# A retrieval layer's gate scatters: only the first head written plainly, seven heads added

## The chip, the cores and the metric

The kernel is one program on one NeuronCore of a Trainium2 chip. The metric is the device time of one execution in microseconds (us), lower is better. Its engines are TensorE (PE: matmuls, with PEld as its weight loads), VectorE (DVE), ScalarE (ACT), GpSimd (POOL) and SyncE (SP, which here only issues DMAs). The core's 16 DMA engines carry the transfers of all of them.

## The reference, cut to what matters

The program computes two transformer blocks over 512 tokens of width 1024. The change touches only the last layer of the second block, a retrieval layer with 16384 experts of one neuron each. Each of 8 heads picks 16 experts per token, with a softmax over its 16 scores as gates:

```python
s1, i1 = lax.top_k(s[:, :, 0], 16); s2, i2 = lax.top_k(s[:, :, 1], 16)
cand = s1[..., :, None] + s2[..., None, :]
cs, ci = lax.top_k(cand.reshape(..., 256), 16)
eidx = jnp.take_along_axis(cidx, ci, axis=-1)      # expert numbers, 0..16383
g = jax.nn.softmax(cs, axis=-1)
a = jax.nn.gelu(hid, approximate=False) * g
return jnp.einsum('chk,chkd->cd', a, vg)
```

Within a head the 16 experts of a token are different. Two heads may pick the same expert for a token, and then both gates count: their sum has to multiply that expert's hidden value.

## The kernel before, in words

**Dense with a gate matrix.** For the first three blocks of 128 tokens (`DENSE = 3`) the kernel doesn't gather rows of the expert tables. It computes the hidden values of all 16384 experts for all tokens, tile by tile (128 tiles of 128 experts), and multiplies them by a gate matrix `gates` in device memory, [expert, expert, token], that is zero wherever no head picked. The gate matrix is cleared early in the program. The fourth block of tokens takes its own way, by gathered rows, and isn't touched by the change.

**The gate scatter.** After each head's picks are known, GpSimd writes them into `gates`. One indirect DMA (`scatter(tb, k)`, lines 971 to 984) writes one element for each of 128 tokens: pick `k` of token block `tb`. A head is 3 x 16 = 48 such DMAs, the eight heads are 384. Line 980 is the plain form (it overwrites the element) for heads 0 to 3 (`PLAIN = 4`), line 983 the adding form (`compute_op=ALU.add`) for heads 4 to 7. The first DMA of a head waits for `s_tk`, which VectorE counts up when the head's gates are set; the first of each token block also waits until all scatters of the heads before it, for that block, have landed (`s_sc[tb]`). Ten scatters of head 0 are issued between GpSimd's last weight splits, the others follow in one sequence, head by head.

**Sums over equal picks.** A plain write overwrites what an earlier head left. So for heads 1 to 3 VectorE first looks up whether an earlier head picked the same expert for the same token, and adds that head's gate (`set_gates`, lines 2050 to 2061). For each of the three token blocks it compares the 16 picks with the 16, 32 or 48 picks of the heads before (line 2056), multiplies by their gates (line 2058), takes the maximum (line 2060) and adds it (line 2061). The copy `earlier` of the pick addresses is kept for this (line 2037).

**The phases around it.** The query projection (kind `wq`) and the key scores end the dense part of the program before this layer. Then comes the *hidden phase* (`hidden`, matmuls at line 1325): for each of 128 tiles, 24 matmuls over weights that SP loads (`load_u`), ScalarE rounds (`high_u`, line 1643) and VectorE completes with the low part (`low_u`, line 1954). ScalarE applies the gelu to the result (`kept_tile`, line 1378) and SP stores it (`keep`, lines 863 and 865). VectorE does the retrieval of heads 2 to 7 (`retrieve`) in the same time, in pieces between the `low_u` of the tiles; the order is written out by hand (`FIRST_LOWS_AT`, `LOWS_AT`): a head is 12 tiles long. ScalarE's exponentials for the softmax come at fixed tiles (`EXP_AT`). PE's code for the hidden phase is one unrolled round of four tiles and then a loop; the code of VectorE and ScalarE is unrolled until the retrieval is done. At the last hidden tile SP waits for all scatters (line 899) and loads the gates of the first four tiles (line 880). Then comes the *output phase* (`outputs`, line 1336), in which PE multiplies gated hidden values by the value table.

Of the kernel before, what the change touches and what calls it, by code (L numbers as in the profile page):

```python
# [24 lines left out]
U32 = mybir.dt.uint32  # L25
I32 = mybir.dt.int32
ALU = mybir.AluOpType
ACT = mybir.ActivationFunctionType
AX = mybir.AxisListType

P = 128
# [3 lines left out]
TB = T // P  # L35
# [11 lines left out]
TOPK = 16  # L47
NT = 128
DENSE = 3
TD = DENSE * P  # L50
PLAIN = 4
LOWS_AT = (1, 2, 1, 2, 1, 2, 1, 2)
FIRST_LOWS_AT = (0, 0, 0, 1, 2, 2, 1, 2)
EARLY = 2
# [348 lines left out]
def program(nc, t_in, out):  # L403
    build_schedule()
    ctx = ExitStack()
    with ctx:
        def sem(name):
            return ctx.enter_context(nc.semaphore(name))
# [40 lines left out]
        expert_gate = [region(o + 2 * P * tb + P, P) for tb in range(TB)]  # L449
        expert_lists = region(o, 2 * P * TB, TB)  # L450
# [57 lines left out]
        def rt(off, n, k=None):  # L508
            return region(TAIL + off, n, k, (tail, TAIL))
# [7 lines left out]
        eq = rt(15360, 1024)  # L517
# [10 lines left out]
        es = rt(19520, 16)  # L528
# [4 lines left out]
        picked = rt(19856, P)  # L533
        rated = rt(19984, P)
        token = rt(20112, 4)
        sum_before = rt(20116, TOPK)
        earlier = rt(20132, DENSE * TOPK * PLAIN, DENSE)
        gf = staged[:, 0:D]
        fss = staged[:, D:D + 16]
        fsq = staged[:, 2 * D:2 * D + 8 * T].rearrange("p (u n) -> p u n", u=8)  # L540
# [96 lines left out]
        s_tk = sem("topk_blocks_done")  # L637
# [41 lines left out]
        sq0, n = {}, 0  # L679
# [12 lines left out]
        auxi, n = {}, 0  # L692
# [45 lines left out]
        for n, (kind, _, loads) in enumerate(PROJ):  # L738
            if kind in SPLIT:
                same = users[kind == "br"]  # L740
# [193 lines left out]
        def _(pool):  # L934
# [36 lines left out]
            def scatter(tb, k):  # L971

                h = k // TOPK
                if tb == 0 and k % TOPK == 0:
                    pool.wait_ge(s_tk, h + 1)
                if h and k % TOPK == 0:
                    pool.wait_ge(s_sc[tb], 16 * k)
                where = bass.IndirectOffsetOnAxis(ap=expert_no[tb][:, k:k + 1], axis=0)
                if h < PLAIN:
                    nc.gpsimd.indirect_dma_start(gate_elements, where, expert_gate[tb][:, k:k + 1], None)\  # L980
                        .then_inc(s_sc[tb], 16)
                else:
                    nc.gpsimd.indirect_dma_start(gate_elements, where, expert_gate[tb][:, k:k + 1], None,  # L983
                                                 compute_op=ALU.add).then_inc(s_sc[tb], 16)
# [3 lines left out]
            for s in STEPS:  # L988
# [14 lines left out]
                elif s[0] == "mem_squares":  # L1003
                    k, mm_, total = s[1], dtmp[:, MEM:2 * MEM], dtmp[:, 0:MEM]
# [723 lines left out]
        def _(dve):  # L1728
            V = nc.vector
            chain = [0]  # L1730

            def link(ins):

                chain[0] += 1
                ins.then_inc(s_d, 1)
                dve.wait_ge(s_d, chain[0])
# [242 lines left out]
            def retrieve(h):  # L1979

                for w in range(2):
                    yield from sorted_half(2 * h + w)
                    yield
                c4 = cand.rearrange("p (t a b) -> p t a b", t=TB, a=16)
                ch = cand.rearrange("p (t n) -> p t n", t=TB)
                shape = [P, TB, 16, 16]
                link(V.tensor_tensor(c4, tva[:, :, 2 * h, :].unsqueeze(3).to_broadcast(shape),
                                     tva[:, :, 2 * h + 1, :].unsqueeze(2).to_broadcast(shape), ALU.add))
                numbers = tif.rearrange("p (t w m) -> p t w m", t=TB, w=2)
                link(V.tensor_copy(numbers, tia[:, :, 2 * h:2 * h + 2, :]))  # L1990
                for tb in range(TB):
                    ins = V.max(cs[:, tb, 0:8], ch[:, tb, :])
                link(ins)
                yield
                for tb in range(TB):
                    ins = V.max_index(ci[:, tb, 0:8], cs[:, tb, 0:8], ch[:, tb, :])
                link(ins)
                for tb in range(TB):
                    ins = V.match_replace(ch[:, tb, :], cs[:, tb, 0:8], ch[:, tb, :], -BIG)
                link(ins)  # L2000
                yield
                for tb in range(TB):
                    ins = V.max(cs[:, tb, 8:16], ch[:, tb, :])
                link(ins)
                V.tensor_tensor(ee[:, h, :].rearrange("p (t k) -> p t k", t=TB), cs,
                                cs[:, :, 0:1].to_broadcast([P, TB, 16]), ALU.subtract).then_inc(s_sm, 1)
                for tb in range(TB):
                    ins = V.max_index(ci[:, tb, 8:16], cs[:, tb, 8:16], ch[:, tb, :])
                link(ins)
                yield  # L2010
                cif = ci.rearrange("p t k -> p (t k)")
                for w in range(2):
                    if w == 0:
                        link(V.tensor_scalar(ca, cif, 4, None, ALU.logical_shift_right))
                    else:
                        link(V.tensor_scalar(ca, cif, 15, None, ALU.bitwise_and))
                    link(V.tensor_copy(cbf[:, w, :], ca))
                    q3 = eq.rearrange("p (r m) -> p r m", m=16)
                    q4 = eq.rearrange("p (t k m) -> p t k m", t=TB, k=16)
                    link(V.tensor_tensor(q3, cbf[:, w, :].unsqueeze(2).to_broadcast([P, 64, 16]),  # L2020
                                         iota16.unsqueeze(1).to_broadcast([P, 64, 16]), ALU.is_equal))
                    link(V.tensor_tensor(q4, q4, numbers[:, :, w, :].unsqueeze(2).to_broadcast(shape), ALU.mult))
                    link(V.tensor_reduce(sel[:, w, :], q3, AX.X, ALU.add))
                    if w == 0:
                        yield
                number, place = cbf[:, 0, :], cbf[:, 1, :]
                ks = slice(TOPK * h, TOPK * (h + 1))
                link(V.scalar_tensor_tensor(number, sel[:, 0, :], float(NKEYS), sel[:, 1, :], ALU.mult, ALU.add))
                for tb in range(TB):
                    part = slice(TOPK * tb, TOPK * (tb + 1))  # L2030
                    ins = V.tensor_scalar(place[:, part], number[:, part], float(TD if tb < DENSE else P),
                                          token[:, tb % DENSE:tb % DENSE + 1], ALU.mult, ALU.add)
                link(ins)
                places = place[:, 0:TOPK * DENSE].rearrange("p (t k) -> p t k", t=DENSE)
                link(V.tensor_copy(expert_lists[:, 0:DENSE, ks].bitcast(U32), places))
                if h < PLAIN:
                    link(V.tensor_copy(earlier[:, :, ks], places))
                link(V.tensor_copy(row_no[:, ks], number[:, TOPK * DENSE:]))
                link(V.tensor_copy(hidden_no[:, ks], place[:, TOPK * DENSE:]))

            def set_gates(h):

                dve.wait_ge(s_ex, h + 1)
                e3 = ee[:, h, :].rearrange("p (t k) -> p t k", t=TB)
                link(V.tensor_reduce(es[:, 0:4], e3, AX.X, ALU.add))
                link(V.reciprocal(es[:, 4:8], es[:, 0:4]))
                ks = slice(TOPK * h, TOPK * (h + 1))
                ins = V.tensor_tensor(expert_lists[:, :, P + TOPK * h:P + TOPK * (h + 1)], e3,
                                      es[:, 4:8].unsqueeze(2).to_broadcast([P, TB, 16]), ALU.mult)
                if 1 <= h < PLAIN:  # L2050
                    n = TOPK * h
                    shape = [P, TOPK, n]
                    same = eq[:, 0:TOPK * n].rearrange("p (k m) -> p k m", k=TOPK)
                    for tb in range(DENSE):
                        link(ins)
                        link(V.tensor_tensor(same, earlier[:, tb, ks].unsqueeze(2).to_broadcast(shape),  # L2056
                                             earlier[:, tb, 0:n].unsqueeze(1).to_broadcast(shape), ALU.is_equal))
                        link(V.tensor_tensor(same, same, expert_gate[tb][:, 0:n].unsqueeze(1).to_broadcast(shape),  # L2058
                                             ALU.mult))
                        link(V.tensor_reduce(sum_before, same, AX.X, ALU.max))  # L2060
                        ins = V.tensor_tensor(expert_gate[tb][:, ks], expert_gate[tb][:, ks], sum_before, ALU.add)  # L2061
                ins.then_inc(s_tk, 1)

            dve.wait_ge(s_kb[3], 16 * 4)
            link(V.tensor_tensor(eq[:, 0:P], ident, iota, ALU.mult))
# [1 line left out]
            for tb in range(1, DENSE):  # L2067
                ins = V.tensor_scalar(token[:, tb:tb + 1], token[:, 0:1], float(P * tb), None, ALU.add)
# [200 lines left out]
```

## Time and profile before

| | us |
|---|---|
| median of 3 runs | 2501.72 (2491.94 to 2502.61) |
| the profiled execution | 2497.29 |
| its span, first to last instruction | 2495.5 |
| PE busy | 2294.9 |
| POOL busy | 1163.1 |
| DVE busy | 1299.1 |
| mean granted TensorE clock | 0.961 of full speed |

Times in the rows below are from the start of the span. The hidden phase begins at 1156 us and ends at 1958 us. "PEclk" is the TensorE clock that was granted, as a share of full speed.

### The profile page before, as it was taken

How to read it: one execution, taken by the hardware profiler on the slowest of the kernel's cores; microseconds unless marked ns; L12 is line 12 of the kernel's file. 1: busy time of each engine (PE TensorE's matmuls, PEld its weight loads, DVE VectorE, ACT ScalarE, POOL GpSimd, SP SyncE). 2: the span in 40 equal slices, each digit the busy share in tenths (PEclk: the TensorE clock that was granted, in tenths of full speed). 3: DMA queues.
4: the chain of work that ended last, by engine and by line, in shares of the span. 5: the costliest groups of instructions: out<-in, count | busy, mean ns of one | idle time of the engine just before them, and what ended most of it. 6: DMA issues, size and time to landing. Idle time of an engine off the chain costs nothing.

```text
span 2495.5 us, 29790 instructions
## 1 busy us (share of the span) xinstructions
PE 2294.9 (92%) x9705; PEld 1779.3 (71%) x9712; DVE 1299.1 (52%) x2403; ACT 901.5 (36%) x1419; POOL 1163.1 (47%) x817
## 2 busy tenths in 40 slices
PE   7999999999999998975596599999999999999998
PEld 5666566787766766764385488888888788888887
DVE  4355433136323563874374366622222488888887
ACT  3554543336434443312121133322222333333333
POOL 3332121244432213375454658888820366555554
PEclk9999999999999999987697799999999999999999
DMA  6554233325321112211242167666643699999997
GB/s 211 190 191 135 70 90 103 95 87 186 114 76 60 43 35 84 70 58 39 64 139 88 55 147 147 144 145 145 135 108 108 228 330 341 355 349 358 355 357 249
DMA packets 208210, 392.32 MB, mean 157 GB/s; under 512 B 56160, under 2 KB 131936, under 8 KB 207872
## 3 DMA queue, kind: packets, MB, share of 16 engines
q1 hardware_dynamic: 151296, 323.89, 39.9%
q0 software_dynamic: 56832, 67.45, 10.8%
q8 instruction: 38, 0.62, 0.1%
q14 instruction: 44, 0.36, 0.0%
HBM read 330.21 MB, written 61.01 MB: 157 GB/s over the span
## 4 chain that ended last, share of the span: by engine, by line
PE 52%; issue 4%; another core or an unknown queue 3%; DVE 1%; ACT 1%; POOL 0%; DMA 0%; DVEq 0%; ACTq 0%; POOLq 0%
PE bank L1325 26%; PE bank L1336 20%; PE bank L1108 5%; PE bank L1304 1%; ACT u_tiles_split L1643 0%; POOL low L1027 0%; PE bank L1314 0%; DMA tail<-hidden_of_last_block,low 0%; DVE low L1784 0%; ACT staged L1378 0%; DVE h_low L1806 0%; DVE tail L2058 0%; DVE tail L2056 0%; DVE tail L2060 0%
## 5 line engine op out<-in xcount | busy, mean ns | idle before, releaser
L1325 PE MATMUL bank<-h_high,u_tiles_split 128*128 128x512 f32 x2048 | 643.8, 394 | 70.5 <-issue 43.9
L950 POOL TENSOR_TENSOR u_split<-blocks,u_split 128x1024 fp32r<-128x1024 f32 (+1 forms) x115 | 283.0, 2461 | 700.0 <-ACT u_split L1471 668.9
L1108 PE MATMUL bank<-h_high,u_split 128*128 128x512 f32 (+1 forms) x1712 | 567.3, 406 | 22.4 <-DVE h_low L1806 17.8
L1336 PE MATMUL bank<-v_split,a_split 128*128 128x512 f32 x2286 | 520.3, 390 | 4.6 <-DVE a_split L2096 4.6
L1325 PEld LDWEIGHTS bank<-h_high,u_tiles_split 128*128 128x128 f32 x2048 | 390.2, 191 | 162.1 <-issue 79.3
L1336 PEld LDWEIGHTS bank<-v_split,a_split 128*128 128x128 f32 x2286 | 430.1, 188 | 94.9 <-DVE v_split L2093 5.4
L1325 PE MATMUL bank<-h_low,u_tiles_split 128*128 128x512 f32 x1024 | 403.7, 394 | 14.6 <-issue 14.4
L1954 DVE TENSOR_TENSOR u_tiles_split<-tail,u_tiles_split 128x1024 fp32r<-128x1024 f32 x128 | 156.6, 1226 | 487.6 <-ACT u_tiles_split L1643 448.4
L1108 PEld LDWEIGHTS bank<-h_high,u_split 128*128 128x128 f32 (+1 forms) x1712 | 324.6, 190 | 110.9 <-issue 23.1
L983 POOL DMA_INDIRECT gates<-low x192 | 314.8, 1640 | 87.2 <-issue 58.2
L1108 PE MATMUL bank<-h_low,u_split 128*128 128x512 f32 (+1 forms) x728 | 287.9, 395 | 0.0
L1027 POOL DMA_INDIRECT low<-in_v,low x128 | 140.2, 1095 | 296.6 <-DVE low L2112 143.6
L980 POOL DMA_INDIRECT gates<-low x192 | 198.4, 1034 | 148.2 <-DVE low L2061 91.5
L1677 ACT CAST v_split<-tail 128x1024 fp32r<-128x1024 f32 x128 | 134.9, 1054 | 300.9 <-PE bank L1336 227.1
L1325 PEld LDWEIGHTS bank<-h_low,u_tiles_split 128*128 128x128 f32 x1024 | 195.4, 191 | 55.7 <-issue 15.7
L1378 ACT ACTIVATE tail<-bank 128x512 f32<-128x512 f32 x96 | 57.4, 598 | 451.3 <-PE bank L1325 223.4
L2093 DVE TENSOR_TENSOR v_split<-tail,v_split 128x1024 fp32r<-128x1024 f32 x128 | 157.0, 1227 | 69.2 <-ACT v_split L1677 56.4
L1035 POOL DMA_INDIRECT tail<-hidden_of_last_block,low x128 | 167.9, 1312 | 43.5 <-issue 38.7
L2112 DVE SCALAR_TENSOR_TENSOR low<-low,tail 128x1024 f32<-128x1024 f32 x128 | 163.8, 1279 | 1.6 <-DMA low<-in_v,low 1.3
L1108 PEld LDWEIGHTS bank<-h_low,u_split 128*128 128x128 f32 (+1 forms) x728 | 138.2, 190 | 33.0 <-issue 6.4
L1643 ACT CAST u_tiles_split<-tail 128x1024 fp32r<-128x1024 f32 x128 | 133.1, 1041 | 8.0 <-DMA tail<-in_uT 6.5
L1856 DVE TENSOR_REDUCE low<-bank 128x1 f32<-128x512 f32 (+3 forms) x112 | 59.7, 535 | 143.1 <-PE bank L1239 71.5
(201 smaller groups left out, 2474.9 us busy)
## 6 DMA issues: line engine op xcount, KB each, us to landing
tail<-in_uT SPq DMA_DIRECT2D x128, 512.0 KB
tail<-in_v SPq DMA_DIRECT2D x128, 512.0 KB
gates<-blocks SPq DMA_DIRECT2D x32, 768.0 KB, 5.8
tail<-gates SPq DMA_DIRECT2D x128, 192.0 KB
kept_hidden<-tail SPq DMA_DIRECT2D x96, 192.0 KB
tail<-kept_hidden SPq DMA_DIRECT2D x96, 192.0 KB
blocks<-in_r SPq DMA_DIRECT2D x24, 512.0 KB, 4.0
blocks<-in_conv SPq DMA_DIRECT2D x16, 512.0 KB, 4.2
```

The source lines that it names most:

```text
L950: nc.gpsimd.tensor_tensor(flat(u, 1)[:, 0:n], ring[:, loads[0] % NW, 0:n], flat(u, 0)[:, 0:n].bitcast(F32), ALU.subtract).then_inc(s_wlo, 1)
L980: nc.gpsimd.indirect_dma_start(gate_elements, where, expert_gate[tb][:, k:k + 1], None)\
L983: nc.gpsimd.indirect_dma_start(gate_elements, where, expert_gate[tb][:, k:k + 1], None, compute_op=ALU.add).then_inc(s_sc[tb], 16)
L1027: nc.gpsimd.indirect_dma_start(rows_in[:, k % 4, :], None, v_rows, bass.IndirectOffsetOnAxis(ap=row_no[:, k:k + 1], axis=0))\
L1035: nc.gpsimd.indirect_dma_start(picked[:, k:k + 1], None, hidden_elements, bass.IndirectOffsetOnAxis(ap=hidden_no[:, k:k + 1], axis=0))\
L1108: last = mm(ps[0:m, :], flat(u, part)[:, k * m:(k + 1) * m], x, start=(k == 0 and j == 0), stop=(k == nk - 1 and j == 2))
L1325: last = mm(bank[slot % 2][:, :], U4[:, slot, w, k, :], x[:, k, :], start=(k == 0 and x is hh and w == 0), stop=(k == KD - 1 and w == 1))
L1336: done = mm(bank[2 + 2 * tb + dh][:, :], A2[:, slot, wa, tb * P:(tb + 1) * P], V2[slot // 2][:, slot % 2, wv, dh * T:(dh + 1) * T], start= ...
L1677: nc.scalar.copy(V2[slot // 2][:, slot % 2, 0], VR[:, slot, :]).then_inc(s_vhi, 1)
L1954: V.tensor_tensor(U4[:, slot, 1].rearrange("p k e -> p (k e)"), UR[:, slot, :], U4[:, slot, 0].rearrange("p k e -> p (k e)").bitcast(F32), ...
L2093: V.tensor_tensor(V2[slot // 2][:, slot % 2, 1], VR[:, slot, :], V2[slot // 2][:, slot % 2, 0].bitcast(F32), ALU.subtract).then_inc(s_vlo, 1)
L2112: V.scalar_tensor_tensor(sparse, rows_in[:, slot, :], rated[:, bass.ds(k, 1)], sparse, ALU.mult, ALU.add).then_inc(s_axpy, 1)
```

## The change

`PLAIN` goes: only head 0 is written plainly, heads 1 to 7 are all scattered with the adding form. VectorE's comparison with earlier heads and its copy of the addresses are taken out.

```diff
@@ def scatter(tb, k)
-                if h < PLAIN:
+                if h == 0:
                     nc.gpsimd.indirect_dma_start(gate_elements, where, expert_gate[tb][:, k:k + 1], None)\
                         .then_inc(s_sc[tb], 16)
                 else:
@@ def retrieve(h)
-                places = place[:, 0:TOPK * DENSE].rearrange("p (t k) -> p t k", t=DENSE)
-                link(V.tensor_copy(expert_lists[:, 0:DENSE, ks].bitcast(U32), places))
-                if h < PLAIN:
-                    link(V.tensor_copy(earlier[:, :, ks], places))
+                link(V.tensor_copy(expert_lists[:, 0:DENSE, ks].bitcast(U32),
+                                   place[:, 0:TOPK * DENSE].rearrange("p (t k) -> p t k", t=DENSE)))
@@ def set_gates(h)
-                ks = slice(TOPK * h, TOPK * (h + 1))
-                ins = V.tensor_tensor(expert_lists[:, :, P + TOPK * h:P + TOPK * (h + 1)], e3,
-                                      es[:, 4:8].unsqueeze(2).to_broadcast([P, TB, 16]), ALU.mult)
-                if 1 <= h < PLAIN:
-                    n = TOPK * h
-                    shape = [P, TOPK, n]
-                    same = eq[:, 0:TOPK * n].rearrange("p (k m) -> p k m", k=TOPK)
-                    for tb in range(DENSE):
-                        link(ins)
-                        link(V.tensor_tensor(same, earlier[:, tb, ks].unsqueeze(2).to_broadcast(shape),
-                                             earlier[:, tb, 0:n].unsqueeze(1).to_broadcast(shape), ALU.is_equal))
-                        link(V.tensor_tensor(same, same, expert_gate[tb][:, 0:n].unsqueeze(1).to_broadcast(shape),
-                                             ALU.mult))
-                        link(V.tensor_reduce(sum_before, same, AX.X, ALU.max))
-                        ins = V.tensor_tensor(expert_gate[tb][:, ks], expert_gate[tb][:, ks], sum_before, ALU.add)
-                ins.then_inc(s_tk, 1)
+                V.tensor_tensor(expert_lists[:, :, P + TOPK * h:P + TOPK * (h + 1)], e3,
+                                es[:, 4:8].unsqueeze(2).to_broadcast([P, TB, 16]), ALU.mult).then_inc(s_tk, 1)
```

## Rows read from the trace of the kernel before

**Rows 1.** The page: PE over the span, and its granted clock in 40 slices.
```profile
PE 2294.9 (92%) x9705; PEld 1779.3 (71%) x9712; DVE 1299.1 (52%) x2403; ACT 901.5 (36%) x1419; POOL 1163.1 (47%) x817
...
PEclk9999999999999999987697799999999999999999
```

**Rows 2.** Busy time by stretch: start:end, length, engines, granted clock, DMA share, GB/s.
```profile
1098.00:1148.00 50.00, 8.31 (x40) 6.92 (x38) 7.46 (x45) 1.69 (x3) 33.91 (x36) 0.61 0.02 1
1156.00:1180.80 24.80, 24.75 (x108) 20.34 (x109) 19.84 (x48) 8.83 (x14) 18.67 (x18) 1.00 0.35 96
1180.80:1225.60 44.80, 12.33 (x26) 6.79 (x26) 1.23 (x1) 1.53 (x2) 30.24 (x31) 0.58 0.07 18
1225.60:1296.40 70.80, 70.80 (x307) 58.47 (x307) 55.81 (x151) 27.40 (x34) 22.92 (x20) 0.98 0.48 145
1296.40:1336.20 39.80, 18.21 (x66) 12.59 (x64) 9.41 (x44) 2.26 (x5) 28.43 (x29) 0.72 0.14 40
1336.20:1386.60 50.40, 49.49 (x207) 40.46 (x208) 40.26 (x99) 16.33 (x21) 18.77 (x17) 0.95 0.48 146
1386.60:1432.20 45.60, 16.68 (x53) 11.50 (x52) 11.42 (x45) 2.81 (x3) 30.82 (x32) 0.68 0.11 29
1455.80:1640.00 184.20, 184.20 (x814) 152.56 (x814) 118.63 (x328) 61.45 (x77) 155.90 (x93) 1.00 0.68 145
1640.00:1828.90 188.90, 188.90 (x835) 156.48 (x834) 42.23 (x38) 53.87 (x70) 158.92 (x99) 1.00 0.66 138
```

**Rows 3.** Who waited for whom, 1180 to 1226 us: us in total, times, longest.
```profile
PE bank L1325 <- issue: 32.4, 14, 17.5
DVE u_tiles_split L1954 <- issue: 31.3, 1, 31.3
```

**Rows 4.** DMA, all queues, 1180 to 1210 us.
```profile
DMA packets 768, 0.01 MB, mean 0 GB/s; under 512 B 768, under 2 KB 768, under 8 KB 768
```

**Rows 5.** DMA, 1450 to 1750 us: all queues, then GpSimd's queue alone.
```profile
DMA packets 45248, 43.50 MB, mean 145 GB/s; under 512 B 24096, under 2 KB 38176, under 8 KB 45243
...
q0 software_dynamic: 21456, 0.09, 19.6%
```

**Rows 6.** POOL in order of time: start, us; first and last scatter of head 1, of heads 4 to 7.
```profile
1156.95 1.69 POOL L980 DMA_INDIRECT gates<-low  x1 [14.37 <-DVE low L2061]
...
1219.23 0.95 POOL L980 DMA_INDIRECT gates<-low  x1 [0.31 <-issue]
...
1455.86 2.36 POOL L983 DMA_INDIRECT gates<-low  x1 [28.99 <-DVE low L2048]
...
1827.37 1.55 POOL L983 DMA_INDIRECT gates<-low  x1 [0.30 <-issue]
```

**Rows 7.** Matmuls of the hidden phase alone (line 1325), by stretch.
```profile
1156.06:1432.22 276.16, 192.25 (x763) 0.82 0.29 86
1640.00:1828.90 188.90, 188.90 (x835) 1.00 0.66 138
```

**Rows 8.** DVE, 1150 to 1460 us, by line and shape: busy us, mean ns.
```profile
L2056 DVE TENSOR_TENSOR tail<-tail 128x768 f32<-128x768 f32 x3 | 2.9, 958 | 0.1
...
L2056 DVE TENSOR_TENSOR tail<-tail 128x512 f32<-128x512 f32 x3 | 2.1, 692 | 0.1
...
L2061 DVE TENSOR_TENSOR low<-low,tail 128x16 f32<-128x16 f32 x9 | 1.6, 174 | 0.3
L2056 DVE TENSOR_TENSOR tail<-tail 128x256 f32<-128x256 f32 x3 | 1.3, 425 | 0.1
```

**Rows 9.** SP's queue in order of time: the loads of the first four gate tiles.
```profile
1954.24 1.78 SPq L880 DMA_DIRECT2D tail<-gates  x4
```

**Rows 10.** All scatters of the adding form: ns min/median/max, first and last start.
```profile
L983 POOL DMA_INDIRECT gates<-low x192: 1552/1559/2612, 1455.9 to 1827.4; - x192
```

**Rows 11.** DVE in order of time: retrieval work from one low part to the next.
```profile
1292.21 0.19 DVE L2016 TENSOR_SCALAR tail<-tail 128x64 uint32<-128x64 uint32 x1
...
1301.77 1.23 DVE L1954 TENSOR_TENSOR u_tiles_split<-tail,u_tiles_split 128x1024 fp32r<-128x1024 f32 x1
```

More of the change, by code:

```diff
@@ L50 @@
 TD = DENSE * P
-PLAIN = 4
 LOWS_AT = (1, 2, 1, 2, 1, 2, 1, 2)
@@ L535, in program @@
         token = rt(20112, 4)
-        sum_before = rt(20116, TOPK)
-        earlier = rt(20132, DENSE * TOPK * PLAIN, DENSE)
         gf = staged[:, 0:D]
```

## The prediction

> **What bounds the kernel now.** I read the page first. PE is busy for 92% of the span, and its clock row is at 9 everywhere except in five slices in the middle, where it falls as low as 6 [rows 1]. So PE sets the time, and the place to look is the one where it is not running. I then asked for busy time by stretch around those slices, moving the borders until each stretch held either a running or a halting PE. The hidden phase falls apart into stretches of two kinds [rows 2]. In three of them (44.8, 39.8 and 45.6 us long) PE does 26, 66 and 53 matmuls at a mean granted clock of 0.58 to 0.72. In the others it does 24 matmuls, one tile, in about 5.5 us. There is one more such halt ahead of the phase, from 1098 to 1148 us, with 40 PE instructions in 50 us.
>
> What does PE wait for there? The view of waits names no engine: the largest entries of PE and of DVE are "issue" (PE 32.4 us in 14 pieces, DVE 31.3 us in one piece) [rows 3]. Every compute engine but POOL stands still at once: DVE 1.23 us of work in 44.8, ACT 1.53, while POOL is busy 30.24 [rows 2]. The DMA view of 30 us inside it shows 768 packets that carry 0.01 MB, nothing else: the loads and stores of the phase have stopped too [rows 4]. POOL's timeline says what these packets are. It issues the plain scatters of head 1 from 1156.95 to 1219.23, 48 of them in 62 us [rows 6]. The halt begins some 24 us after the first and ends some 5 us after the last. The second and third halt lie in the same way in heads 2 and 3, and the 50 us ahead of the phase in head 0.
>
> The contrast is in the same trace. From 1455.86 to 1827.37 POOL issues the 192 scatters of heads 4 to 7, the adding form [rows 6]. The two stretches that hold them show PE at 184.20 of 184.20 and 188.90 of 188.90 us, at clock 1.00, beside 138 to 145 GB/s [rows 2]. GpSimd's queue takes 19.6% of the DMA engines there, for 0.09 MB [rows 5], so these writes are not free, but nothing waits for them. Nor is it the form of the code: PE has been in its loop since the fifth tile, and the code of VectorE and ScalarE is still unrolled at head 4 and 5, while DVE is busy for 118.63 of 184.20 us [rows 2]. I conclude that the plain element scatters, at this rate, halt the chip's other queues, and the adding ones don't. What exactly in the chip fills up, the trace doesn't show.
>
> **The change, step by step.** The sum is made against the profiled execution, 2497.3 us; the median of the runs is 4.4 us above it.
>
> *The halts of heads 1 to 3 go.* From the first hidden matmul to the end of the third halt, 276.16 us, PE does 763 matmuls [rows 7]. The undisturbed rate is 188.90/835 = 0.2262 us [rows 7], the same with busy DVE (184.20/814 = 0.2263) [rows 2]. 763 of them take 172.6 us. The halts and their slow clock cost 276.2 - 172.6 = 103.5 us. For the adding form at heads 1 to 3 there is no row; the bounds are no halt (the 373 us of adds at heads 4 to 7) and the same halt (plain at heads 1 to 3). I take no halt, because the nearest rows are the same instruction, the same 48 per head, beside the same loads and the same VectorE work.
>
> *The scatters get slower.* A plain scatter follows the last after (1219.23 - 1156.95)/47 = 1.33 us, an adding one after (1827.37 - 1455.86)/191 = 1.945 us [rows 6]. Beside a busy DVE it is 184.20/93 = 1.98 [rows 2]. POOL gets 144 x 0.65 = 94 us more. Nobody waits for a single scatter; what waits is SP, which at the last hidden tile needs all of them before it loads gates, now at 1954.24 [rows 9]. With the phase 103.5 us shorter that is 1850.7. Head 1's gates are set 4.4 us earlier (next step), so its first scatter is at 1152.5. 144 at 1.98 end at 1437.6, where head 4's gates are long ready: by the order in `LOWS_AT` they are set behind the low part of tile 25, at the latest near 1156 + 27 x 5.43 = 1303. Then 192 at 1.945 end at 1811. That leaves 40 us. This is cover, not gain: behind the scatters POOL has only work that waits for the last hidden tile anyway. Without the cover each 0.1 us per scatter would cost 34 us.
>
> The Trainium skill (SBUF — State Buffer, the section on its two separate sides) warns that GpSimd is kept from writing DMA descriptors while VectorE uses the port pair that they share. By that the scatters beside the retrieval would be spaced out more. The trace bears it out by little: 1.98 us beside the busy DVE against 188.90/99 = 1.91 beside the idle one [rows 2].
>
> *VectorE loses the sums.* Per token block there are three passes and a short add: three blocks at 16, 32 and 48 earlier picks are 3 x (3 x 0.425 + 0.174) = 4.4, 3 x (3 x 0.692 + 0.174) = 6.8 and 3 x (3 x 0.958 + 0.174) = 9.1 us [rows 8]; the passes of lines 2058 and 2060 are taken to be as long as that of 2056. With some 0.2 us for each of four copies this is 21 us. I count it as nothing. It hides behind matmuls: in the stretch that holds head 2's sums PE runs 70.80 of 70.80 us and DVE 55.81 [rows 2]. Only head 3's, the longest, may have cost PE the 0.9 us that it lacks in the next running stretch, which the 103.5 already contain.
>
> *What doesn't move.* Head 0 stays plain, so the 50 us before the phase stay. The output phase has the same work. The sum is 2497.3 - 103.5 = 2393.8; I say 2394.
>
> **The rivals.**
>
> *VectorE comes late once PE doesn't halt (0.10).* Its longest stretch of retrieval between two low parts is 1301.77 - 1292.21 = 9.6 us [rows 11], longer than a tile of 5.4. If nothing were made ahead, heads 2 and 3 would lose 4.2 us each and the start of the retrieval in the phase some more: about 2402 to 2410. Against it: heads 4 to 7 have the same order and lose nothing [rows 2].
>
> *The adds halt partly (0.05).* In heads 1 to 3 half of the gain is kept: 2394 + 52 = 2446. For it: they follow at once on head 0's plain writes, which no row shows. Against it: head 4's adds follow head 3's plain writes after 29 us [rows 6] and PE stays full.
>
> *POOL becomes the bound (0.04).* The scatters end after SP needs them when one takes more than (1850.7 - 1152.5)/336 = 2.08 us, against 1.945 to 1.98 now: at 2.2 us the time is 2394 + 41 = 2435. To cost more than before takes over 2.38 us each. The longest single add took 2.61 us [rows 10]; with 0.30 of issue between two, 336 of these would give 2394 + 279 = 2673, the far bound. The rows of heads 4 to 7 hold 192 of them, busy and idle neighbours included, and none of the stretches is near 2.08.
>
> *The adds halt everything as well (0.05, the other side).* If the small writes as such are the cause, a head's halt grows with its scatters. Halts now cost 34.5 us per head; adds take 30 us longer per head, all of it behind the first 24 us, so each halt becomes 64 us: 2497 + 90 = 2587. It decides as soon as the adds of a head halt for longer than the plain ones did. The Trainium skill (DMA: Bandwidth & Descriptors, Specifications) speaks for this: transfers under 512 B are done by reading, modifying and writing, which would make plain and adding elements alike. The rows of heads 4 to 7 contradict it as a cause of halts.
>
> **How the numbers follow.** The forecast has 0.76: 2394, its own range 2384 to 2404 (the runs before scatter by 11 us). The range of 8 in 10 adds the late VectorE and a part of the partial halt: 2380 to 2430; above it lie most of the partial halt, half of the POOL-bound case and the other side, some 0.12, below it 0.02. About 0.5%, 12 us, is what a measurement can tell from no change. Faster takes the first four cases without the POOL-bound tail: 0.94. The other side and that tail give slower 0.05, and 0.01 is left for no difference.
>
> **What would show it.** PE runs without a break from 1156 us on, and the hidden phase ends near 1854. Only 48 plain scatters are left, with one halt at 1098 to 1148. The adds follow each other every 1.9 to 2.0 us, from about 1152 to 1811, and SP's first gate load comes near 1851, not later than the last tile asks. PE's clock row loses its dip but for head 0's slices. It is wrong if PE's "issue" waits come back in heads 1 to 3, if SP's gate load waits for the last scatter, or if PE waits for line 1954 in the first 20 tiles.

## The result

| | kernel before | changed kernel |
|---|---|---|
| median, us | 2496.83 (2487.37 to 2502.61, 4 runs) | 2399.56 (2396.45 to 2403.02, 4 runs) |
| the profiled execution, us | 2497.29 | 2401.24 |
| its span, us | 2495.5 | 2399.4 |
| mean granted clock | 0.961 | 0.976 |

The ratio is 0.9614, 95% interval 0.9576 to 0.9653. On this occasion, whose chip isn't known, the change saves 97 us. The experiments ran on four chips that are named below by their numbers, and on three of them there was nothing to save: there the kernel before itself takes 2347 to 2349 us. So the profile after is read first as it is, and then the other chips.

**The page of the changed kernel:** PE over the span and the granted clock. Of the dip of five slices [rows 1] two slices are left.

```profile
PE 2277.0 (95%) x9705; PEld 1772.5 (74%) x9712; DVE 1273.5 (53%) x2363; ACT 901.0 (38%) x1419; POOL 1256.1 (52%) x817
...
PEclk9999999999999999997799999999999999999999
```

**Changed kernel, busy time by stretch** (start:end, length, PE, PEld, DVE, ACT, POOL, clock, DMA share, GB/s). These answer to [rows 2].

```profile
1098.00:1148.00 50.00, 15.61 (x79) 13.94 (x77) 13.31 (x49) 5.59 (x8) 38.53 (x38) 0.63 0.03 1
1148.00:1164.70 16.70, 0.00 (x0) 0.00 (x0) 0.00 (x0) 1.09 (x3) 13.96 (x10) 0.50 0.23 0
1164.70:1351.60 186.90, 186.86 (x815) 154.59 (x816) 121.79 (x368) 63.82 (x82) 157.95 (x96) 0.99 0.65 139
1351.60:1535.00 183.40, 183.40 (x811) 151.84 (x810) 119.42 (x330) 60.86 (x77) 155.36 (x93) 1.00 0.67 144
1535.00:1803.00 268.00, 268.00 (x1184) 221.93 (x1183) 60.66 (x52) 75.41 (x98) 223.88 (x139) 1.00 0.63 131
```

PE runs without a break through the stretches that hold the adds of heads 1 to 3, beside as busy a VectorE as before. The halt of head 0 has stayed, and it has grown: it now lasts until 1164.7, and in its last 17 us no compute engine but POOL does anything worth the name. DMA share is 0.23 there with 0 GB/s: from 1149 to 1163 us all 1152 packets are GpSimd's, so what the DMA engines do is adds.

**Changed kernel, the chain that ended last** (the work that set the time, each piece followed back to what released it). The whole hidden phase is one piece of 3072 matmuls.

```profile
1138.71 24.89 another core or an unknown queue
1163.61 1.08 ACT low L1660 x2
1164.74 698.64 PE bank L1322 x3072
```

**Changed kernel, POOL and SP in order of time:** the last plain scatter, the first and the last add, the first loads of gates. They answer to [rows 6, 9].

```profile
1143.98 0.96 POOL L977 DMA_INDIRECT gates<-low  x1 [0.30 <-issue]
1145.25 1.62 POOL L980 DMA_INDIRECT gates<-low  x1 [0.30 <-issue]
...
1799.40 1.57 POOL L980 DMA_INDIRECT gates<-low  x1 [0.32 <-issue]
...
1859.53 1.78 SPq L877 DMA_DIRECT2D tail<-gates  x4
```

The mean time between starts is (1799.40 - 1145.25)/335 = 1.953 us, and the scatters end 58 us before SP asks for them.

**The balance of the two profiled executions.** The hidden phase takes 698.6 instead of 1958.13 - 1156.06 = 802.1 us: -103.4. It begins at 1164.7 instead of 1156.1: +8.7. What lies behind it takes 536.0 instead of 537.4: -1.4. The sum is -96.1 us, and 2497.3 - 2401.2 = 96.1.

### The profile page after: what moved, and what is told of

Same layout as the page of the kernel before. It is cut to its first block, busy times and chain, and to the rows that moved or that the text cites. A ratio compares the mean times of both kernels' runs of the same rounds, so it can differ in the third digit from the quotient of the medians.

```text
span 2399.4 us, 29750 instructions
## 1 busy us (share of the span) xinstructions
PE 2277.0 (95%) x9705; PEld 1772.5 (74%) x9712; DVE 1273.5 (53%) x2363; ACT 901.0 (38%) x1419; POOL 1256.1 (52%) x817
## 4 chain that ended last, share of the span: by engine, by line
PE 55%; another core or an unknown queue 3%; DVE 1%; ACT 0%; POOL 0%; issue 0%; DMA 0%; DVEq 0%; POOLq 0%
PE bank L1322 29%; PE bank L1333 21%; PE bank L1105 5%; PE bank L1301 1%; POOL low L1024 0%; DMA tail<-hidden_of_last_block,low 0%; DVE low L1781 0%; ACT staged L1375 0%; DVE h_low L1803 0%; ACT u_tiles_split L1640 0%; POOL tail L1032 0%; DVE low L2126 0%; PE bank L1189 0%; ACT blocks L1375 0%
## 5 line engine op out<-in xcount | busy, mean ns | idle before, releaser
L1322 PE MATMUL bank<-h_high,u_tiles_split 128*128 128x512 f32 x2048 | 632.3, 390 | 22.3 <-ACT low L1660 22.3
L980 POOL DMA_INDIRECT gates<-low x336 | 553.6, 1648 | 102.4 <-issue 102.4
L1322 PEld LDWEIGHTS bank<-h_high,u_tiles_split 128*128 128x128 f32 x2048 | 385.4, 188 | 102.7 <-ACT low L1660 22.5
L1951 DVE TENSOR_TENSOR u_tiles_split<-tail,u_tiles_split 128x1024 fp32r<-128x1024 f32 x128 | 156.9, 1226 | 420.4 <-ACT u_tiles_split L1640 410.6
L1024 POOL DMA_INDIRECT low<-in_v,low x128 | 145.5, 1137 | 221.4 <-DVE low L2093 135.1
L2074 DVE TENSOR_TENSOR v_split<-tail,v_split 128x1024 fp32r<-128x1024 f32 x128 | 157.0, 1226 | 68.0 <-ACT v_split L1674 53.0
L1468 ACT CAST u_split<-blocks 128x1024 fp32r<-128x1024 f32 (+1 forms) x115 | 119.7, 1041 | 23.8 <-PE bank L1127 23.8
```

The lines of the kernel that those rows point to most:

```text
L1024: nc.gpsimd.indirect_dma_start(rows_in[:, k % 4, :], None, v_rows, bass.IndirectOffsetOnAxis(ap=row_no[:, k:k + 1], axis=0))\
L1322: last = mm(bank[slot % 2][:, :], U4[:, slot, w, k, :], x[:, k, :], start=(k == 0 and x is hh and w == 0), stop=(k == KD - 1 and w == 1))
L1951: V.tensor_tensor(U4[:, slot, 1].rearrange("p k e -> p (k e)"), UR[:, slot, :], U4[:, slot, 0].rearrange("p k e -> p (k e)").bitcast(F32), ...
L2074: V.tensor_tensor(V2[slot // 2][:, slot % 2, 1], VR[:, slot, :], V2[slot // 2][:, slot % 2, 0].bitcast(F32), ALU.subtract).then_inc(s_vlo, 1)
```

## The experiments

### Which half of the change does it (chip 11)

Four kernels ran on chip 11, where the kernel before took 2489.12 us (2477.47 to 2497.60, 7 runs). The changed kernel itself wasn't run there, and the kernel before has no trace from there; its rows are from the first occasion.

**Adds, with VectorE's sums kept** (in the kernel before; gates that two of the first four heads share are counted too often).

```diff
-                if h < PLAIN:
+                if h == 0:
                     nc.gpsimd.indirect_dma_start(...)
```

> The kernel before with one half of the change: heads 1 to 3 are scattered with the adding form, VectorE still makes the sums over equal picks (so gates that two of the first four heads share are counted too often; the time alone is of interest). Theory A (the plain scatters halt the other queues, the sums are hidden): as the changed kernel, 2400 us, at most 3 us above it, hidden phase without a halt. Rival B (part of the gain is VectorE's 21 us of sums): 2410 to 2421 us, with PE waiting for line 1954 near heads 2 and 3.

Measured: 2391.53 us (2388.43 to 2392.04), ratio 0.9601 (0.9558 to 0.9643), beside 0.9614 for the whole change on the first occasion. The scatters' form alone gives the whole gain. The sums cost PE a fraction of a microsecond: in the 17 us that hold head 3's, PE runs 16.25, and the view of waits puts 0.8 us down to line 1954.

```profile
1155.40:1281.00 125.60, 125.55 (x554) 103.94 (x555) 95.43 (x279) 43.78 (x59) 105.13 (x63) 1.00 0.63 138
1281.00:1298.00 17.00, 16.25 (x72) 13.14 (x70) 14.88 (x24) 5.28 (x8) 14.56 (x9) 1.00 0.61 140
```

**Plain, without the sums** (in the changed kernel; a later head overwrites an equal pick's gate instead of adding to it).

```diff
-                if h == 0:
+                if h < 4:
                     nc.gpsimd.indirect_dma_start(...)
```

> The other half alone: heads 0 to 3 plain as before, VectorE's sums and its copy of the addresses taken out (a gate of an earlier head is then overwritten instead of added to). Theory A: as before, 2490 to 2500 us, with the three halts of 30 to 40 us in heads 1 to 3. Rival B: 2475 to 2480 us.

Measured: 2537.07 us (2535.15 to 2544.96), ratio 1.0197 (1.0149 to 1.0245). Neither side had this: taking the sums out made it slower by 48 us. The chain shows where, and a stretch of the halt shows that nothing but POOL runs in it:

```profile
1138.13 77.75 another core or an unknown queue
1215.91 1.08 ACT low L1660 x2
1217.04 88.77 PE bank L1322 x384
```

```profile
1150.00:1205.00 55.00, 0.00 (x0) 0.00 (x0) 0.00 (x0) 0.00 (x0) 41.83 (x44) 0.50 0.02 0
```

The hidden phase begins at 1217 instead of 1156. The timeline of POOL shows head 1's plain scatters directly behind head 0's, 0.30 us apart, where in the kernel before POOL had waited 14.37 us for line 2061 [rows 6]. With nothing between the two heads the halt of head 0 goes on through head 1. Heads 2 and 3 halt here too. The same shows on a small scale between the two kernels with adds, though from two occasions: with the sums POOL stood 14.18 us between the heads and the phase began at 1155.4; without them, in the changed kernel, at 1164.7. That the gap is the reason is argued from these pairs; no kernel has the gap without the sums.

### Rate or kind (chip 11)

**One small memset behind each plain scatter** (in the kernel before; nothing left out).

```diff
                         .then_inc(s_sc[tb], 16)
+                    if h or tb or k >= 10:
+                        if pads[0]:
+                            pool.wait_ge(s_pad, pads[0])
+                        nc.gpsimd.memset(pad[:, 0:PADN], 0.0).then_inc(s_pad, 1)
+                        pads[0] += 1
```

> The kernel before, with a small memset on GpSimd behind each plain scatter (but for the ten early ones), so that plain scatters follow each other about as slowly as adding ones do (1.26 us between starts becomes 1.6 to 1.9). Nothing is left out. Theory A1 (it is the rate of the plain scatters: something fills up because they are issued faster than they drain): the halts of heads 1 to 3 and that of head 0 vanish or shrink to under 10 us, 2340 to 2420 us. Theory A2 (it is the kind of write, at any such rate): the halts stay and last longer, since a head's scatters take longer: 2520 to 2600 us.

Measured: 2437.03 us (2433.83 to 2448.14), ratio 0.9802 (0.9753 to 0.9851): between the two theories. The memset spaced the starts by less than meant, since it fits mostly into the 0.30 us that pass between two scatters anyway:

```profile
1269.05 0.96 POOL L984 DMA_INDIRECT gates<-low  x1 [0.16 <-issue]
1270.00 0.23 POOL L989 MEMSET tail<- 128x128 f32 x1
1270.40 1.23 POOL L984 DMA_INDIRECT gates<-low  x1 [0.16 <-issue]
```

The median between starts went from 1.26 us to 1.35. The means of whole heads differ more. The first and last starts of heads 1 and 2:

```profile
1143.61 0.96 POOL L984 DMA_INDIRECT gates<-low  x1 [0.17 <-issue]
...
1208.67 0.96 POOL L984 DMA_INDIRECT gates<-low  x1 [0.17 <-issue]
1266.97 1.70 POOL L984 DMA_INDIRECT gates<-low  x1 [57.11 <-DVE low L2070]
...
1338.07 1.23 POOL L984 DMA_INDIRECT gates<-low  x1 [0.17 <-issue]
```

Head 1 has (1208.67 - 1143.61)/47 = 1.38 us, head 2 (1338.07 - 1266.97)/47 = 1.51, and head 3, which follows at once on head 2, 1.50. In the kernel before, heads 1 to 3 have 1.33, 1.38 and 1.34. Yet the halts of heads 2 and 3 are gone but for 2 us. Head 2's is the last of these stretches; the first is head 1's, still a halt, behind head 0's:

```profile
1162.00:1212.60 50.60, 19.58 (x37) 11.11 (x38) 5.58 (x15) 3.06 (x4) 42.23 (x70) 0.53 0.12 32
1212.60:1270.00 57.40, 57.35 (x242) 47.17 (x242) 41.17 (x114) 19.81 (x25) 2.87 (x3) 0.95 0.45 142
1270.00:1316.00 46.00, 46.00 (x204) 38.10 (x203) 38.23 (x122) 15.26 (x20) 40.89 (x62) 1.00 0.50 148
```

So plain writes as a kind are not enough for a halt: 96 of them in a row, heads 2 and 3, cost PE 2 us. The two halts that stay are those of the heads with the faster starts. But a halt also makes the starts faster, as nothing runs beside POOL in it, so the means of whole heads mix cause and effect: by POOL's timeline the first 20 gaps of head 2 are 1.49 us on average in the kernel before, which halts, and 1.51 here. A rate is the likely reason and isn't pinned down; nor did a kernel with plain scatters as slow as adds meet a chip that halts.

### The last halt (chip 11)

**Head 0 added too** (in the changed kernel; nothing left out).

```diff
-                if h == 0:
+                if h < 0:
                     nc.gpsimd.indirect_dma_start(...)
```

> The changed kernel with head 0 added as well (the gate matrix is cleared long before). Nothing is left out. Theory A: the last halt, from 1104 to 1164 us in the changed kernel, goes too. PE does some 16 us of work in it, so 45 us are to be had: 2355 us. GpSimd then has 374 adds from about 1092 us on, which at 1.95 us end at 1821, a few us after SP would load the first gates (1860 - 45 = 1815), so up to 10 us of it may be given back: 2355 to 2365 us. Rival C (that halt is of the phase's start, code loading or the first weights, and not of the plain scatters): 2400 us or a little more.

Measured: 2364.15 us (2363.36 to 2364.97), ratio 0.9494 (0.9453 to 0.9536). Rival C falls: with no plain scatter there is no halt, the first hidden matmul is at 1108.7. And here GpSimd is the bound at the end. POOL's last add, SP's loads of gates and PE's first output matmul:

```profile
1820.00 1.55 POOL L980 DMA_INDIRECT gates<-low  x1 [0.30 <-issue]
...
1823.05 1.75 SPq L877 DMA_DIRECT2D tail<-gates  x4
...
1829.17 3.33 PE L1333 MATMUL bank<-v_split,a_split 128*128 128x512 f32 x7 [23.86 <-DVE a_split L2077]
```

PE stands for 23.9 us between the phases, where it stood 2.7 us in the kernel before. The adds end where they were expected (1821); it was PE that came earlier than reckoned, so some 21 us are given back, not 10. It is the fastest kernel run on chip 11, 27 us ahead of the adds with sums. On a chip without halts it wasn't run. An estimate: it has no halt to lose, so it should take the same 2364 us there, some 19 us more than the 2345 of the changed kernel on chip 3 (below).

### Then another chip: no halts at all (chips 4, 3 and 2)

The next four kernels went to chip 4. The kernel before took 2347.32 us there (2342.52 to 2351.56, 7 runs), 142 us less than on chip 11. They had been meant to tell how the halt comes about, and without halts none of the four can.

**Three memsets behind each plain scatter**, the same edit with a loop of three.

> As the paced run, with three small memsets behind each plain scatter instead of one: one memset made 1.26 us between starts only 1.35 and the halts of heads 2 and 3 were nearly gone, those of heads 0 and 1 were not. Three should give 1.9 to 2.2 us, no faster than adding scatters. Nothing is left out. Theory A1 (rate): no halt in any head, also not in head 0; the phase then starts near 1110 us; with VectorE's sums still in it, 2345 to 2365 us. Theory A2 (kind): halts of heads 0 and 1 as long as a head's scatters, 2430 us or more.

Measured: 2367.97 us, ratio to the kernel before 1.0095 (1.0074 to 1.0116). Starts are 1.87 us apart in the median. Of the halt it says nothing. But it puts a price on the rival in which POOL is the bound: the last scatter starts at 1823.8, SP's loads of gates come at 1826.97 instead of some 1803, and PE stands for 26.2 us:

```profile
PE bank L1346 <- DVE a_split L2106: 26.2, 1, 26.2
```

So scatters that end some 22 us too late cost 21 us, about one for one, as the prediction had it.

**At most four plain scatters under way** (in the kernel before; nothing left out). Four semaphores in turn take the place of `s_sc` for the plain ones:

```diff
+                if h < PLAIN:
+                    n = plain_no[0]
+                    plain_no[0] += 1
+                    if n >= OPEN:
+                        pool.wait_ge(s_ro[n % OPEN], 16 * (n // OPEN))
...
-                        .then_inc(s_sc[tb], 16)
+                        .then_inc(s_ro[n % OPEN], 16)
```

> The kernel before, with at most four plain scatters under way: each waits until the one four before it has landed, and a head's first until all earlier ones have. Nothing is left out. Theory A1a (the plain writes land more slowly than they are issued and pile up in the DMA engines or behind them): GpSimd is now held to the pace of landing, more than 1.26 us between starts, nothing piles up, halts are gone or under 10 us each: 2350 to 2430 us. Theory A1b (they land at once, and it is the making of descriptors at this rate that starves the others): the waits end at once, starts stay 1.26 us apart and the halts stay: 2480 to 2500 us.

Measured: 2344.23 us (one run), beside 2347. On a chip without halts the waits for landings cost nothing. POOL waited for a landing five times in 192, 7.8 us in all; three of the five, 6.9 us, are the first scatters of heads 1 to 3, which wait for all earlier ones, so the limit of four held POOL up twice, for 1.0 us:

```profile
POOL gates L991 <- issue: 53.8, 177, 0.3
POOL gates L991 <- DMA gates<-low: 7.8, 5, 2.6
```

So here a plain scatter nearly always lands within the 5 us in which four are issued. Behind the last one of head 0 the landing is seen 3.1 us after its start.

**The plain scatters of heads 1 to 3 side by side** (in the kernel before; the gates of these heads land in 6144 neighbouring elements, the wrong place).

```diff
+                    if h:
+                        c = TOPK * tb + k % TOPK
+                        where = bass.IndirectOffsetOnAxis(ap=near[:, c:c + 1], axis=0)
                     nc.gpsimd.indirect_dma_start(gate_elements, where, expert_gate[tb][:, k:k + 1], None)\
```

> The kernel before, with the plain scatters of heads 1 to 3 written to 6144 elements that lie side by side instead of to the picked ones (the gates of these heads are then in the wrong place; the time alone is of interest). Same number, size and rate of writes. Theory A3 (it is scattered addresses in device memory that make the writes slow): no halts in heads 1 to 3, 2400 us, head 0's halt stays. Theory A4 (the number of small elements alone counts): as before, 2480 to 2500 us.

Measured: 2427.97 us (one run), 81 us more than the kernel before on this chip. A3 had neighbouring addresses as the cheap ones; they are the dear ones. Heads 1 to 3 also write the same 6144 elements three times over, so whether it is the neighbourhood or the repetition isn't told apart. But it isn't the halt of chip 11. The view of DMA issues from 1160 to 1400 us (count, KB, median us from issue to landing) shows slow loads in this kernel:

```profile
tail<-in_uT SPq DMA_DIRECT2D x30, 512.0 KB, 13.4
```

In the kernel before on chip 3, in the same window, and in the kernel with four under way on this same chip 4, from 1145 to 1350 us:

```profile
tail<-in_uT SPq DMA_DIRECT2D x44, 512.0 KB, 3.7
```

```profile
tail<-in_uT SPq DMA_DIRECT2D x37, 512.0 KB, 3.7
```

ScalarE waits for the loads by name here, VectorE and PE wait behind it, and the DMA engines are busy (share 0.81 from 1160 to 1400 us):

```profile
ACT u_tiles_split L1649 <- DMA tail<-in_uT: 170.1, 29, 12.2
```

In the halts the DMA engines are idle ([rows 2, 4], and a share of 0.02 in the 55 us on chip 11 above), and no load is named. SP doesn't issue any for 42 us there. Its loads around the first halt of the hidden phase, in the kernel before on the first occasion:

```profile
1177.08 0.01 SPq L858 DMA_DIRECT2D tail<-in_uT  x1
...
1219.27 0.70 SPq L858 DMA_DIRECT2D tail<-in_uT  x1
```

The Trainium skill (DMA: Bandwidth & Descriptors, Specifications) says that transfers under 512 B are done by reading, modifying and writing. That small writes can hurt large transfers beside them this kernel bears out (13.4 against 3.7 us). That they do so by being small alone it doesn't, as the same writes spread over `gates` left the loads at 3.7 us. Whether neighbouring writes hinder each other in being read and modified no run shows.

**Sixteen plain scatters in heads 1 to 3, then adds** (in the changed kernel; an equal pick's gate in token block 0 is overwritten).

```diff
-                if h == 0:
+                if h == 0 or (h < 4 and tb == 0):
                     nc.gpsimd.indirect_dma_start(...)
```

> The changed kernel with the first 16 scatters of heads 1, 2 and 3 (token block 0) plain again, the other 32 adding (a block-0 gate of an earlier head is then overwritten instead of added to). In the kernel before a head's halt began 19 to 22 scatters into the head. Theory A1 (something fills over some 20 plain scatters in a row, and only then is there a halt): heads 2 and 3 show no halt, as nothing was full before them; head 1 follows directly on head 0 and may lengthen its halt by up to 20 us: 2395 to 2420 us. Rival (every plain scatter takes its share from the others): a third of the halts stays, 2430 us.

Measured: 2348.18 us (one run) beside 2347.32. No halt was there to be had with either kernel, so it tells nothing on the question.

**The two kernels once more (chip 3).**

> The changed kernel as it is. On the chip of the last four runs the kernel before took 2347 us, 142 to 150 us less than on the two occasions ahead of them, and plain scatters showed no halt. Theory H (whether plain scatters at 1.26 us halt the other queues hangs on the chip or on where the run's memory lies, not on the kernel): where the kernel before takes 2480 to 2500 us, this takes 2390 to 2403 us; where it takes some 2347 us, nothing is there to gain. Then the phase starts near 1114 us, the scatters end at 1142 + 336 x 1.945 = 1796 us, and SP's load of gates comes at 1805 us, so they are still hidden, if by 9 us only: 2343 to 2352 us, the same as before. Rival G (the adds cost something of their own beside PE): 2355 to 2370 us there.

> The kernel before once more, for its profile on this chip. Theory H: either three halts of 30 to 45 us in the hidden phase, one ahead of it, 2480 to 2500 us; or none, PE without a break from some 1114 us on, 2342 to 2352 us. Nothing between the two.

Measured: changed 2345.47 us (2340.63 to 2348.74, 10 runs), before 2348.92 us (2342.55 to 2352.33, 13 runs), ratio 0.9986 (0.9974 to 0.9999); the profiled run of the kernel before took 2342.56 us. Theory H holds: no difference by the 0.5% that the prediction set as its bound. The page and the stretches of the kernel before on this chip, with the borders of [rows 2]:

```profile
PE 2266.4 (97%) x9705; PEld 1763.8 (75%) x9712; DVE 1299.0 (55%) x2403; ACT 900.4 (38%) x1419; POOL 1169.3 (50%) x817
...
PEclk9999999999999999999999999999999999999999
```

```profile
1098.00:1148.00 50.00, 46.98 (x230) 39.09 (x229) 40.33 (x117) 23.57 (x32) 38.96 (x37) 1.00 0.33 98
...
1180.80:1225.60 44.80, 44.80 (x200) 37.08 (x199) 37.45 (x116) 15.09 (x19) 35.05 (x33) 1.00 0.50 145
```

Where PE did 26 matmuls on the first occasion it does 200 here, beside 33 plain scatters instead of 31. POOL's scatters have the same length (minimum 954 ns in both) and the same 0.30 us between them:

```profile
L980 POOL DMA_INDIRECT gates<-low x192: 954/962/1786, 1058.5 to 1340.3; - x192
```

The kernel before now has two traces, and they place the difference between the occasions. The hidden phase begins at 1106.07 here instead of 1156.06, 50.0 us earlier, and is some 103 us shorter; the spans differ by 2495.5 - 2340.8 = 154.7 us.

In the changed kernel on this chip the cover of the adds is thin: the last one starts at 1799.80, and SP's loads come at 1803.23, 3.4 us later.

```profile
1799.80 1.57 POOL L980 DMA_INDIRECT gates<-low  x1 [0.30 <-issue]
...
1803.23 1.78 SPq L877 DMA_DIRECT2D tail<-gates  x4
```

**Four under way, twice more (chips 3 and 2)**, for the case that one of them halts.

> At most four plain scatters under way, once more, for the case that this chip halts. If it does: theory A1a (plain writes land more slowly than they are issued and pile up): starts spread beyond 1.26 us, GpSimd waits for landings, halts gone or under 10 us each, 2340 to 2400 us; theory A1b (they land at once, the making of descriptors starves the others): starts stay 1.26 us apart, halts stay, 2480 to 2500 us. If this chip doesn't halt: 2344 us as before.

> At most four plain scatters under way, once more, since two chips in a row showed no halt in the kernel before. If this chip halts (the kernel before at 2480 to 2500 us): theory A1a (plain writes land more slowly than they are issued and pile up) gives starts spread beyond 1.26 us, GpSimd waiting for landings, no halts or such under 10 us each, 2340 to 2400 us; theory A1b (they land at once, and the making of descriptors at this rate starves the others) gives starts 1.26 us apart, halts as before, 2480 to 2500 us. If this chip doesn't halt either: 2344 us, as the kernel before.

Measured: 2344.17 us (one run) on chip 3, and on chip 2 2345.77 us (2341.66 to 2350.36, 10 runs) beside 2347.88 us for the kernel before, ratio 1.0000 (0.9989 to 1.0010). Neither chip halts.

## Why the prediction was right, and where it was not

*The halts of heads 1 to 3 go.* Right, in place and size: 103.5 us forecast, 103.4 measured. That it is the form of the scatters and not the sums is shown by the two half changes on chip 11, and that no plain scatter means no halt by the kernel that only adds. That the first occasion's halts are the same thing as chip 11's is taken from their likeness: in the same heads, with no wait that is named, 2497 and 2489 us.

*The same halt stays ahead of the phase.* This is the step that failed: "Head 0 stays plain, so the 50 us before the phase stay." The phase began 8.7 us later instead; less the 1.4 us gained behind it, that is the 7 us between the forecast 2394 and the profiled 2401.2. With the sums out, the adds of head 1 follow head 0's plain scatters without a gap, and the halt outlasted the last plain scatter by 20 us (1143.98 to 1163.6) instead of 6. How adds prolong a halt that they don't start isn't shown. It was even foreseen as a question ("they follow at once on head 0's plain writes, which no row shows"), but placed in heads 1 to 3 and not ahead of them.

*The scatters get slower, and stay covered.* Right: 1.953 us against 1.945 to 1.98 forecast; SP's load at 1859.5 is the forecast 1850.7 and the 8.7 us of later start. The cover was larger than the 40 us reckoned (58), as head 1 began earlier and the phase later. That it is cover and nothing else is shown by the kernel that only adds, which lost it. The spacing depends on VectorE as little as before: 183.40/93 = 1.97 us beside the retrieval, 268.00/139 = 1.93 without. The Trainium skill (SBUF — State Buffer, the section on its two separate sides) warns that GpSimd is kept from writing descriptors while VectorE uses the port pair that they share; by these rows that is worth 0.04 us per scatter here.

*The sums are hidden.* Right on chip 11. Where PE never halts they do show a little: the kernel before on chip 3 loses 2.0 us waiting for line 1954, the changed kernel none.

```profile
PE bank L1325 <- DVE u_tiles_split L1954: 2.0, 2, 1.2
```

*The conclusion behind it all* was that "the plain element scatters, at this rate, halt the chip's other queues". As a cause it stood every test made on chip 11, which halts in the same way. As a sentence on the kernel it is too wide. The same kernel with the same scatters shows no halt on chips 4, 3 and 2. No rival had the halts as a property of the chip or of the place of the run; the three runs from before the change, which agreed within 0.5%, had looked like enough. So the number came true in part by luck: on chip 4, 3 or 2 there would have been nothing to save.

**What stays open.** Why chip 11 (and the first occasion, whose chip isn't known) halts and the others don't: the chip itself, or where the run's memory lies, no run tells apart. What it is that comes to a stop there: all other DMA traffic ended 18, 22 and 19 scatters into heads 1, 2 and 3 (near 1180, 1300 and 1390 us), the engines wait on "issue", which means on nothing that the profile shows, and two of four halts went when the starts were spaced a little more. This looks like a queue that fills when it drains a little more slowly than scatters come, and a PE that halts within a tile, on "issue", looks like instructions that don't arrive. Both are argued, not shown; the kernel that limits the writes under way was made for it and never met a chip that halts.

## What to carry to other kernels

An engine that is idle on "issue" together with all others, while one queue sends many tiny writes, points at the writes and not at the work around them; changing their form or their rate is worth a run before anything is tuned in the schedule. Before a large gain is believed, time both kernels on more than one chip: this change was worth 4% on the first occasion and nothing on chip 3. And taking a piece of work away can pull two bursts together that it had kept apart: without the sums, the kernel with plain scatters took 48 us more on chip 11.

## What the runs showed of the hardware that was not expected

- The kernel before takes 2489 us on chip 11 and 2347 to 2349 us on chips 4, 3 and 2, each within 1% of itself. By the traces of the first occasion and of chip 3 the difference lies in the four halts: 50 us before the hidden phase and some 103 in it, of 154.7.
- A plain element scatter occupies GpSimd for 0.96 us and an adding one for 1.56 (medians), each with 0.30 us behind it; on GpSimd's queue they are 32 and some 142 packets (4608 packets for 144 plain scatters between 1150 and 1450 us of the kernel before, 21456 for 151 adds [rows 5]).
- 128 x 144 element writes into 6144 neighbouring elements came with 13.4 us for the 512 KB loads beside them on chip 4; spread over `gates`, they came with 3.7 us on chips 4 and 3.
- In a halt on chip 11 no engine but GpSimd executed anything for 55 us, at a DMA share of 0.02.
- A halt can outlast the plain scatters by 20 us when adds follow at once (the changed kernel, first occasion).
